# Contiguous PSUM writes in the gate and second transform stage, and gate rows stored 128 at a time

## The reference, cut to what matters

```python
def fourier_mixer(h, w_in, w_out):          # h: (B, S, D), w_in: (D, 2E), E = 2048
    proj = h @ w_in
    xin, z = proj[..., :D_INNER], proj[..., D_INNER:]
    xg = xin.reshape(b, s, N_GROUPS, GROUP_DIM).astype(jnp.float32)   # 8 groups of 256 channels
    y = jnp.fft.fft2(xg, axes=(1, 3), norm="ortho").real
    y = y.astype(h.dtype).reshape(b, s, D_INNER)
    return (y * jax.nn.silu(z)) @ w_out
...
for i in range(DEPTH):
    h = rms_norm(x, norms[i])
    x = x + mixers[i % N_MIXERS](h, *params[i])
return rms_norm(x, final_norm)
```

## Time and profile before

| what | value |
|---|---|
| median of 6 runs | 2056.89 us (2035.15 to 2345.82) |
| the profiled execution, its own time | 2035.27 us |
| its span, first to last instruction | 2033.7 us |
| spans of the eight cores | 2015.2 to 2033.7 us |
| TensorE matmul (PE) busy | 1822.6 us, 90% of the span |
| VectorE (DVE), ScalarE (ACT) busy | 805.8 us (40%), 720.6 us (35%) |
| DMA mean | 101 GB/s, queue q1 153.50 MB, q0 51.12 MB |
| chain that ended last | PE 80%, DMA 12% |

### The profile page before, as it was taken

How to read it: one execution, slowest core, us unless ns; L and a number is a source line. 1 busy time by engine, 2 the same in 40 slices (tenths; PEclk the granted TensorE clock), 3 DMA queues, 4 the chain that set the end, 5 groups by cost and what they waited for, 6 DMA issues and landing times.

```text
span 2033.7 us, 25797 instructions; the slowest of 8 cores (2015.2 to 2033.7 us)
## 1 busy us (share of the span) xinstructions
PE 1822.6 (90%) x8845; PEld 873.4 (43%) x8976; DVE 805.8 (40%) x1278; ACT 720.6 (35%) x1170; POOL 71.2 (4%) x137
## 2 busy tenths in 40 slices
PE   5999989999999303699979999999999999999997
PEld 2333642544345301344444444444444444444443
DVE  5540620220121300244334455555545554555554
ACT  4441511221222100133334444544454445444442
POOL 2110000000000002000000000000000000000000
PEclk9999999999999756899999999999999999999999
DMA  8647591552658119978753010111011011101111
GB/s 248 184 142 161 70 148 29 100 91 39 107 89 110 65 44 278 315 221 264 245 189 117 27 52 27 52 53 47 32 52 52 37 42 53 52 27 53 52 48 42
DMA packets 82639, 206.27 MB, mean 101 GB/s; under 512 B 7360, under 2 KB 35136, under 8 KB 79040
## 3 DMA queue, kind: packets, MB, share of 16 engines
q1 hardware_dynamic: 56976, 153.50, 23.4%
q0 software_dynamic: 25536, 51.12, 15.3%
HBM read 168.10 MB, written 88.15 MB: 126 GB/s over the span
## 4 chain that ended last, share of the span: by engine, by line
PE 80%; DMA 12%; another core or an unknown queue 4%; DVE 2%; issue 1%; ACT 1%; SPq 0%; POOL 0%; DVEq 0%; ACTq 0%; POOLq 0%
PE pf L807 33%; PE pf L424 19%; PE pf L883 11%; PE pf L703 8%; PE pf L564 4%; DMA x1d<-b0x 4%; DMA wb_82<-wbT 2%; DMA b0gy<-gy 2%; DMA zrow<-sz_72 1%; PE pb L870 1%; PE pf L854 1%; DMA wz_77<-wz 1%; DMA a0x_53<-xt 1%; PE pf L539 1%
## 5 line engine op out<-in xcount | busy, mean ns | idle before, releaser
L807 PE MATMUL pf<-Win,b1h 128*128 128x512 bf16 x3008 | 667.1, 380 | 10.6 <-DMA b1h<-h1d 7.1
L807 PEld LDWEIGHTS pf<-Win,b1h 128*128 128x128 bf16 x3072 | 300.0, 98 | 364.6 <-issue 11.1
L703 PE MATMUL pf<-W,b0gy 128*128 128x512 bf16 x998 | 226.5, 382 | 103.9 <-DMA b0gy<-gy 102.6
L883 PE MATMUL pf<-W,b1g1T 128*128 128x512 bf16 x992 | 221.9, 382 | 8.7 <-DVE b1x L894 3.9
L823 DVE BATCH_NORM_STATS2 b1st<-b1v 128x6 f32<-128x512 f32 x128 | 88.8, 694 | 271.9 <-ACT b1v L820 271.9
L703 PEld LDWEIGHTS pf<-W,b0gy 128*128 128x128 bf16 x1024 | 99.6, 99 | 218.4 <-issue 106.6
L859 DVE SCALAR_TENSOR_TENSOR b1sz<-pf,gTs,b1u 128x256 bf16<-128x256 f32 x256 | 123.8, 484 | 93.3 <-PE pf L854 69.2
L883 PEld LDWEIGHTS pf<-W,b1g1T 128*128 128x128 bf16 x1024 | 100.7, 98 | 123.0 <-issue 10.6
L424 PE MATMUL pf<-hT,wz_79 128*128 128x512 bf16 x320 | 142.4, 644 | 4.1 <-ACT sz_73 L428 4.1
L424 PE MATMUL pf<-hT,wz_77 128*128 128x512 bf16 x320 | 140.3, 637 | 2.1 <-DMA wz_77<-wz 2.1
L424 PE MATMUL pf<-hT,wz_78 128*128 128x512 bf16 x320 | 139.2, 633 | 0.0
(11 more groups left out here) (154 smaller groups left out, 1591.1 us busy)
## 6 DMA issues: line engine op xcount, KB each, us to landing
b0x<-x SPq DMA_DIRECT2D x32, 512.0 KB, 5.4
x1d<-b0x SPq DMA_DIRECT2D x32, 512.0 KB, 6.4
b1x<-x1d SPq DMA_DIRECT2D x32, 512.0 KB, 3.3
out<-b1x SPq DMA_DIRECT2D x32, 512.0 KB, 2.6
b0gy<-gy SPq DMA_DIRECT2D x7, 2048.0 KB, 11.2
wind<-l_w_in POOLq DMA_DIRECT2D x12, 1024.0 KB, 31.9
Win<-wind POOLq DMA_DIRECT2D x12, 1024.0 KB, 66.0
V<-ud SPq DMA_DIRECT2D x32, 256.0 KB, 17.0
```

The source lines that it names most:

```text
L703: pe.op(lambda e: e.matmul(bank[:], gt[:, kc, c0:c0 + 128], W0[:, kc, nh * 512:(nh + 1) * 512], start=(kc == 0), stop=(kc == 15)), gbs + [ ...
L807: pe.op(lambda e: e.matmul(bank[:], h1[sl][:, kc, :], Win[:, kc, fb * 512:(fb + 1) * 512], start=(kc == 0), stop=(kc == 7)), [h1b[sl], Win ...
L883: pe.op(lambda e: e.matmul(bank[:], g1t[sl][:, kc, :], W1[:, kc, nh * 512:(nh + 1) * 512], start=(kc == 0), stop=(kc == 15)), [g1tb[sl][kc ...
```

## The change

In a zgroup the matmuls write the bank straight through, place t*64+p, and ACT reads it permuted: consecutive values are 64 floats apart. In the second stage each of the four matmuls writes its own 128 places, and the evacuation becomes two instructions of 256 values, one for each c, which read the bank in runs of two (k) with the next j 128 floats on. The second gate tile is stored with all 128 rows, its row 0 with a value that is not wanted; the DMA of the 8 rows of `szsp` therefore moves behind the last of these stores and waits for all of them (`waw=True`).

```diff
@@ zgroup
                 bank, bb = next_f()
-                ho = bank[:].rearrange("c (p t) -> c t p", t=8)
                 for dc in range(8):
                     mv = hT[:, dc, b8 * 1024:(b8 + 1) * 1024].rearrange("d (t p) -> d t p", p=128)
-                    pe.op(lambda e: e.matmul(ho, w[:, dc, :], mv[:, :, hf * 64:hf * 64 + 64],
+                    pe.op(lambda e: e.matmul(bank[:], w[:, dc, :], mv[:, :, hf * 64:hf * 64 + 64],
...
                 act.op(lambda e: e.activation(out=ov_[:, hf * 64:hf * 64 + 64, b8 * 8:b8 * 8 + 8],
-                                              in_=bank[:].rearrange("c (p t) -> c p t", t=8),
+                                              in_=bank[:].rearrange("c (t p) -> c p t", t=8),
@@ second stage
                         pr = 4 * qd + jj
-                        o = bank[:].rearrange("d (c t j k) -> d j c t k", c=2, t=32, j=4)[:, jj]
+                        o = bank[:, jj * 128:(jj + 1) * 128]
...
-                    scaled(ev_engine(), H[:, qd, dc, :, 0:256], bank[:].rearrange("d (c k) -> d c k", c=2), sc,
-                           [bb, g0sb], [Hb[qd]], 512)
+                    q = ev_engine()
+                    for cs in range(2):
+                        scaled(q, H[:, qd, dc, cs, 0:256].rearrange("d (t j k) -> d t j k", j=4, k=2),
+                               bank[:].rearrange("d (j c t k) -> d c t j k", c=2, j=4, k=2)[:, cs], sc,
+                               [bb, g0sb], [Hb[qd]], 256)
@@ gate
-                    sp.dma(gyT[r0 + h:r0 + 128, :], o[h:128].rearrange("c a b -> c (a b)"), d_gy[i], reads=[ob],
+                    sp.dma(gyT[r0:r0 + 128, :], o[:].rearrange("c a b -> c (a b)"), d_gy[i], reads=[ob],
                            writes=[gyTb])
@@ groups
                     gate_tile(szsp, szspb, p128, p128b, p128, p128b)
-                    sp.dma(gyT.rearrange("(g r) s -> g r s", r=256)[:, 128, :],
-                           szsp[:].rearrange("c a b -> c (a b)"), d_sp, reads=[szspb], writes=[gyTb])
+            sp.dma(gyT.rearrange("(g r) s -> g r s", r=256)[:, 128, :],
+                   szsp[:].rearrange("c a b -> c (a b)"), d_sp, reads=[szspb], writes=[gyTb], waw=True)
             barrier()
```

More of the change, by code:

```diff
@@ L536, in build @@
                         pr = 4 * qd + jj
-                        o = bank[:].rearrange("d (c t j k) -> d j c t k", c=2, t=32, j=4)[:, jj]
+                        o = bank[:, jj * 128:(jj + 1) * 128]
                         m = bd0 if pr == 0 else bd
-                        pe.op(lambda e: e.matmul(o, V[:, pr, dc * 128:(dc + 1) * 128],
-                                                 m.rearrange("r (c t k) -> r c t k", c=2, t=32),
-                                                 start=(jj == 0), stop=(jj == 3)),
+                        pe.op(lambda e: e.matmul(o, V[:, pr, dc * 128:(dc + 1) * 128], m, start=(jj == 0), stop=(jj == 3)),
                               [Vb[qd], cpkb], [bb], waw=False, inc=(jj == 3))
-                    scaled(ev_engine(), H[:, qd, dc, :, 0:256], bank[:].rearrange("d (c k) -> d c k", c=2), sc,
-                           [bb, g0sb], [Hb[qd]], 512)
+                    q = ev_engine()
[3 more added lines that the diff above has]
+                               [bb, g0sb], [Hb[qd]], 256)
                     if qd == 0:
```

## The result

The changed kernel takes 1797.75 us (median of 10 runs), the kernel before 2044.27 us (median of 20): the ratio is 0.881, interval 0.878 to 0.884. Lowest against lowest it is 1794.12 against 2035.15 us. The forecast was 1774 us with a range of 1745 to 1812: the direction and the size hold, but some 20 us of the gain are missing. The medians are of all runs, while the ratios leave out those in which cores show a lower granted clock and take longer, and the profiled execution has such a stretch behind stage A (0.81 from 650 to 775 us on core 0; cores 0 and 1 have spans of 1819.0 and 1818.8 us, the other six 1779.5 to 1792.7), so of cores 0 and 1 only stage A is used.

The account below looks back on a forecast made before the run. PE's gate matmuls, dear for their output pattern, and one-engine 127-row stores were taken as the bound. Terms -34 - 7 - 163 + 5 + 2 - 4 - 13 - 47.5 = -261.5 from 2035.3 give 1774 us, range 1745 to 1812.

Parts of the forecast that it names:

- forecast case: The prediction's main case: 1774 us, own range 1750 to 1795, chance 0.68.
- loop with zgroups: 24 loop steps with a zgroup: 4.31 us a step become 2.9, -34 us (-39 to -29).
- last 8 zgroups and the wait for wz: Ahead of zall(4): 27.5 us become 13.9, but PE stalls 9 us (5 to 12) for wz; net -7 us.
- second stage: Bound by its evacuations on ACT and DVE; two halves cost more fixed time: +5 us, bounds 0 and +25.
- fold(2): PE stalls 8 us against 6 before for its weights, queued behind precasts: +2 us (-6 to +14).
- `last_column`: Its 11.85 us wait and slow pq(7) come of a zrow store behind a 127-row store: -13 us (-13 to -6).
- the end: Stage A's end: 57.0 us from last store issue to first load shrink, -47.5 us (-51 to -38).
- the store that isn't faster: Rival, chance 0.03: the 128-row store is no faster, so the tail and both waits stay: 1843 us.
- the input rival: Rival, chance 0.03: gate matmuls are slow for reading hT in 64-element pieces; only the stores count: 1976 us.
- the DMA rival: Rival, chance 0.11: precasts a quarter slower, fold(2) waits 10 us more, barrier 7: 1791 us; sign: PE waits over 10 us.
- Dear reads: Rival, chance 0.12: a permuted value costs ACT and DVE twice; second stage +25 instead of +5: 1794 us.
- the slower case: Rival, chance 0.03: ACT's permuted read bounds all 128 zgroups, slower above 3.76 us an evacuation; at 4.5 us, 2130 us.

Follow-up runs that it names:

- experiment 4: Changed kernel with the second gate tile stored without row 0, as rows 1 to 120 and 121 to 127, szsp store back at g = 6: 1799.46 us, ratio 0.881.
- Experiment 5: Changed kernel with the loop's square and norm of tile s+2 issued ahead of the evacuation of zgroup s: 1782.18 us, ratio 0.871.
- experiment 6: Changed kernel with the last zgroups in order 0, 3, 1, 2, so the load of wz_4 is issued earlier: 1794.34 us, ratio 0.877.
- experiment 7: Changed kernel with the same 16 precasts in another order, two of 1 MB in the first group: 1789.01 us, ratio 0.874.
- experiment 1: Kernel before with the zgroup part alone, 127-row stores and second stage as they were: ratio 0.966, lowest 1974.21 us.

## Why the prediction was right, and where its sum was not

The time lies in the stated range of 1745 to 1812, but above the forecast case's own 1750 to 1795: it was the room left for the rivals that held it. The mechanism was right; most errors of the single terms go the same way and make the missing 20 us. The terms against core 0 of the two profiled executions, cut where the same instruction starts in both timelines of PE:

| term | forecast us | measured us |
|---|---|---|
| start up to the first zgroup | 0 | +1.7 |
| loop with zgroups | -34 | -24.6 |
| last 8 zgroups and the wait for wz | -7 | -2.9 |
| `zall(4)` | -13.6 | -11.8 |
| second stage | +5 | +4.2 |
| `zall(5)`, pq(1), fold(2) | -13.6 + 2 | -8.8 |
| ten `zall`, the wait at `zall(6)` | -136 - 4 | -143.8 |
| pq(6), `last_column`, pq(7) | -13 | -7.1 |
| the end | -47.5 | -48.5 |
| sum | -261.5 | -241.7 |

- **What PE pays for.** Right for the gate: the price follows the output pattern. The input's pattern (`hT` in pieces of 64) is unchanged and a gate matmul costs 216 ns; that rival (1976 us) is out. So is the store that isn't faster (1843), by 8.5 us at the end and by experiment 4.
- **The second stage** was misread, at no cost to the sum. Its 74 ns, or 0.58 ns per column, are not the price of writing pairs: 24 matmuls fill six banks, and 1.78 us is 0.297 us a bank, the pace of the evacuations (0.311). Where no bank is waited for, pairs take 57 ns, as straight writes do. So the 0.58 ns contradict nothing: the pairs are free, only single floats 8 apart pay, and that stage is no argument against the input rival. The term of +5 us came out at +4.2 because it took the stage as bound by its evacuations.
- **The loop** was mis-sized: 3.36 us a step instead of 2.9. I had compared how busy each engine is and allowed a little for imperfect overlap. What set the step was the order on one of them: ACT, though not full, takes the evacuation ahead of a square on which three engines wait. Experiment 5 gives all of it back and more.
- **The wait for wz**, taken as 9 us from 5 to 12, was 12.5: the load landed 18.6 us after its issue, not 15 to 17, with two weight loads ahead of it and the loads of `V` beside it. Issued ahead of those two, in experiment 6, it landed after 11.1. A wait of over 10 us for wz was the prediction's own sign of the DMA rival, and it came true, though 9 of the 12.5 us stood in the sum. That `zall(4)` then gained 1.8 us less belongs to the wait too: PE idled, the granted clock was 0.50 (1.2 GHz) from 147.6 to 151 us, and 64 matmuls took 15.84 us. After the 1.5 us wait of experiment 6 the clock stayed at 1.00 (2.4 GHz) and they took 13.97.
- **fold(2)** got 8 us of stall in the sum; it has 1.2. The precasts did delay something, but not what I named: the stall fell on `zall(5)`, 9.85 us, at the store of gate tile 0. I had costed that store in the queue ahead of the weights and not asked who waits for it. This is the DMA rival's mechanism at another place: what a shrunk group no longer covers becomes a wait. Its 1791 us is nearer to the result than my 1774.
- **`last_column`**: the `zrow` store behind a 127-row store explained 7 of the 11.85 us. The 4.8 left come of the last precasts (experiment 7 makes these 4 MB instead of 6, and the wait is gone); I had called them just hidden, and only looked at the barrier.
- **Reads.** A permuted read costs nothing that a row shows. Gate evacuations of before and after, and the second stage's halves in the timelines of ACT and DVE after:

```profile
L428 ACT ACTIVATE sz_74<-pf x24: 597/597/598, 61.7 to 542.6; 128x512 bf16<-128x512 f32 x24
```

```profile
L427 ACT ACTIVATE sz_74<-pf x24: 597/597/597, 57.2 to 397.5; 128x512 bf16<-128x512 f32 x24
```

```profile
164.03 15.41 ACT L524 ACTIVATE H<-pf,g0s 128x256 bf16<-128x256 f32 x42
```

```profile
164.51 18.50 DVE L526 TENSOR_SCALAR H<-pf,g0s 128x256 bf16<-128x256 f32 x46 [42.95 <-PE pf L538]
```

Two halves take 0.73 us on ACT and 0.80 on DVE, as forecast (0.73 and 0.82) from the rows' own slope and a second instruction's fixed time; no row parts that fixed time from a small price of the permuted halves, but the gate's evacuations show none. Dear reads (1794) and the slower case, which needed 3.76 us an evacuation, are out, though 1794 is near the time that was measured: a total cannot tell two causes apart, the row of the disputed instruction can.

## What to carry to other kernels

When one engine's work shrinks, look for what its length had been hiding: here a 57 us store with a group of 71 us over it cost little, and most of the gain until it went too; each edit alone brought 70 us, both 240. Price a matmul by its output pattern, and read that price where nothing is waited for: a series that looks unbroken can hold waits, as the second stage's 74 ns did. Put the permutation on the read of the engine that has time. When a loop falls below its old bound, follow one step through the order of each engine's queue, not only through how busy the engine is.

## What the runs showed of the hardware

- A matmul that writes PSUM in single floats 8 apart takes 429 ns per 512 columns, straight through 216; pairs of floats 8 apart take 57 ns per 128 columns, the same as straight through.
- ACT reads PSUM one float from every 256 bytes in the same 597 ns per 512 values as straight through.
- One store on one DMA engine can hold a core's whole DMA at 19 to 28 GB/s while loads of other queues are wanted (PE waited 97.7 us for `wb` in experiment 1). With stores of 120 and 7 rows it waited 1.6 us for them (experiment 4, 100 to 520 us).
